# A transformer block of two stages on one core: the rows of x loaded and transposed three weight tiles later, and the modulation chunks weighed on another timetable

## What is computed

```python
c_act = jax.nn.silu(c)
mod = c_act @ w_ada[l] + b_ada[l]                        # (1, 6*2048): shifts, scales, gates
sh1, sc1, gt1, sh2, sc2, gt2 = jnp.split(mod[:, None, :], 6, axis=-1)
h = rmsnorm(x, g_mix[l]) * (1.0 + sc1) + sh1
x = x + gt1 * hybrid_mixer(h, w_in[l], ...)              # pooling, attention, LRU, w_out
h = rmsnorm(x, g_ffn[l]) * (1.0 + sc2) + sh2
x = x + gt2 * conv_glu_ffn(h, ...)
# second block, per layer: memory keys and values
mkv = mem @ w_mem_kv
# keys are normalised per head, transposed, and used by an attention over 256 memory rows
```

## Time and profile before

| | |
|---|---|
| median of 3 runs | 3042.99 us (3042.93 to 3043.94) |
| profiled execution, its own time | 3042.21 us |
| its span in the trace | 3040.4 us |
| TensorE busy | 3020.1 us, 99% |
| VectorE busy | 1970.1 us, 65% |
| ScalarE busy | 1492.6 us, 49% |
| bytes moved | 658.20 MB |

### The profile page before, as it was taken

How to read it: one execution, slowest core, us unless ns; L and a number is a source line. 1 busy time by engine, 2 the same in 40 slices (tenths; PEclk the granted TensorE clock), 3 DMA queues, 4 the chain that set the end, 5 groups by cost and what they waited for, 6 DMA issues and landing times.

```text
span 3040.4 us, 38832 instructions
## 1 busy us (share of the span) xinstructions
PE 3020.1 (99%) x14556; PEld 2533.0 (83%) x14556; DVE 1970.1 (65%) x2078; ACT 1492.6 (49%) x1797; POOL 15.1 (0%) x32
## 2 busy tenths in 40 slices
PE   8999999999999999999999999999999999999999
PEld 6899888888888888888888888888888888888887
DVE  7989987875665568675555656565475555566564
ACT  6555456444444445554444354545454454444543
POOL 0000000000000000000000000000000000000000
PEclk9999999999999999999999999999999999999999
DMA  9998988865555556555555455555455555445454
GB/s 397 416 379 300 365 333 296 311 220 189 190 187 188 189 182 221 175 180 178 190 177 194 161 173 194 174 186 183 163 180 179 193 173 193 166 169 190 170 182 171
DMA packets 167272, 658.20 MB, mean 216 GB/s; under 512 B 18594, under 2 KB 18914, under 8 KB 154722
## 3 DMA queue, kind: packets, MB, share of 16 engines
q1 hardware_dynamic: 163554, 634.85, 59.3%
q0 software_dynamic: 3584, 21.48, 1.9%
HBM read 654.14 MB, written 2.11 MB: 216 GB/s over the span
## 4 chain that ended last, share of the span: by engine, by line
PE 91%; DVE 5%; DMA 3%; ACT 1%; issue 0%; SPq 0%; DVEq 0%; ACTq 0%
PE pg L1194 27%; PE pg L1196 27%; PE pg L1195 27%; DVE R L1765 2%; DMA w_raw<-w 2%; DVE w_lo L1821 2%; PE pm L1229 1%; DMA R<-w_ada 1%; PE pm L1257 1%; PE pm L1652 1%; PE pg L1280 1%; PE pg L1282 1%; PE pg L1281 1%; DVE x_rows L1765 0%; PE pm L1546 0%
## 5 line engine op out<-in xcount | busy, mean ns | idle before, releaser
L1701 DVE TENSOR_TENSOR w_lo<-w_raw,w_hi 128x1024 fp32r<-128x1024 f32 x868 | 1061.3, 1225 | 948.7 <-ACT w_hi L626 944.3
L626 ACT ACTIVATE w_hi<-w_raw 128x1024 fp32r<-128x1024 f32 x868 | 919.7, 1060 | 1294.0 <-PE pg L1196 1287.2
L1194 PE MATMUL pg<-w_hi,hT_hi 128*128 128x512 f32 x2912 | 1146.0, 394 | 4.6 <-DVE w_lo L1821 4.2
L1196 PE MATMUL pg<-w_hi,hT_lo 128*128 128x512 f32 x2912 | 1135.5, 390 | 0.0
L1195 PE MATMUL pg<-w_lo,hT_hi 128*128 128x512 f32 x2912 | 1134.7, 390 | 0.0
L1194 PEld LDWEIGHTS pg<-w_hi,hT_hi 128*128 128x128 f32 x2912 | 547.8, 188 | 120.7 <-issue 5.8
L1196 PEld LDWEIGHTS pg<-w_hi,hT_lo 128*128 128x128 f32 x2912 | 547.3, 188 | 115.1
L1195 PEld LDWEIGHTS pg<-w_lo,hT_hi 128*128 128x128 f32 x2912 | 547.9, 188 | 110.3
L1194 PE MATMUL pg<-w_hi,y_parts 128*128 128x512 f32 x864 | 337.6, 391 | 0.0
L1196 PE MATMUL pg<-w_hi,y_parts 128*128 128x512 f32 x864 | 336.4, 389 | 0.0
L1195 PE MATMUL pg<-w_lo,y_parts 128*128 128x512 f32 x864 | 336.1, 389 | 0.0
(11 more groups left out here) (313 smaller groups left out, 1940.0 us busy)
## 6 DMA issues: line engine op xcount, KB each, us to landing
w_raw<-w SPq DMA_DIRECT2D x1008, 512.0 KB, 4.0
R<-w_ada SPq DMA_DIRECT2D x59, 1024.0 KB, 9.0
x_rows<-w_ada SPq DMA_DIRECT2D x18, 1024.0 KB, 9.1
R<-w_ada POOLq DMA_DIRECT2D x11, 1024.0 KB, 7.3
R<-w SPq DMA_DIRECT2D x16, 512.0 KB, 11.0
R<-w_ada SPq DMA_DIRECT2D x10, 512.0 KB, 7.4
R<-mem_T SPq DMA_DIRECT2D x8, 512.0 KB, 9.2
x_rows<-x SPq DMA_DIRECT2D x4, 1024.0 KB, 13.0
```

The costliest lines, as they stand in the source:

```text
L626: act.activation(w_hi[:, g % RING, :, :].rearrange("p c n -> p (c n)"), raw[:, g % RING, :], ACT.Copy).then_inc(hi_done, 1)
L1194: pe.matmul(out, hi, w_hi[:, slot, c, :], start=start, stop=False)
L1196: return pe.matmul(out, lo, w_hi[:, slot, c, :], start=False, stop=stop)
L1701: tt(flat(w_lo[:, g % RING, :, :]), raw[:, g % RING, :], flat(w_hi[:, g % RING, :, :]).bitcast(F32), ALU.subtract).then_inc(lo_done, 1)
```

## The change

It does six things. (1) X_FROM goes from 14 to 16, and the six places that serve from there on come in the order x, x, 14, 16, 4, 6. (2) WEIGH_FEEDS: sixteen chunks are fed behind tiles 4 to 23 (thirteen behind 5 to 21 before), the other sixteen behind tiles 24 to 43 (nineteen behind 24 to 45 before), and six chunks of a later group go one tile later, behind 114 to 124 instead of 113 to 123. (3) SP loads the two halves of x behind tiles 11 and 13 instead of 7 and 8; ScalarE's squares, VectorE's row_norm and TensorE's transposes of x follow three tiles later. (4) The sums of squares of mk0 are turned into roots before row_norm instead of after it, mem_normed(0) goes from 15 to 17, and the transposes of mk0 from behind tile 16 to behind tile 19; ScalarE's copy of them stays at `upto(21)`. (5) The first two chunks in the buffer of x, now 16 and 17, are loaded at turns 23 and 24 (before: 14 and 15, at turns 22 and 23). (6) TensorE transposes the probabilities of head h one tile later.

```diff
--- before.py
+++ after.py
@@ -29,7 +29,7 @@
 ADA = 6 * D
 AH = D // 2
 X_HOME = 19
-X_FROM, X_TO, X_LEFT = 14, 32, 56
+X_FROM, X_TO, X_LEFT = 16, 32, 56
 RAW_DEEP, RAW_DEEP_TO = RING + 1, 80
 LAYERS = 2
 LEVELS = 9
@@ -89,7 +89,7 @@
     if n < X_FROM:
         first = (14, 16, 4, 6)[n % 4]
     elif n < X_TO:
-        first = (X_HOME, X_HOME + 2, 4, 6, 14, 16)[(n - X_FROM) % 6]
+        first = (X_HOME, X_HOME + 2, 14, 16, 4, 6)[(n - X_FROM) % 6]
     elif n < X_LEFT:
         first = (X_HOME, X_HOME + 2, 14, 16)[(n - X_TO) % 4]
     else:
@@ -477,10 +477,9 @@
 
         P_MEM0, P_MIX, P_Y, P_MEM1, P_FF = 0, 4, 12, 20, 28
         FRONT_SSQ = TB + TB * NB
-        LATE = ((52, 3, 5), (57, 5, 8), (65, 7, 9), (74, 5, 11), (85, 17, 28), (113, 6, 12), (136, 5, 11))
-        FIRST = 13
-        WEIGH_FEEDS = [5, 6, 8, 9] + [11 + 12 * n // 9 for n in range(FIRST - 4)]
-        WEIGH_FEEDS += [24 + 23 * n // (EARLY - FIRST) for n in range(EARLY - FIRST)]
+        LATE = ((52, 3, 5), (57, 5, 8), (65, 7, 9), (74, 5, 11), (85, 17, 28), (114, 6, 12), (136, 5, 11))
+        WEIGH_FEEDS = [4, 5, 6, 7, 9, 10, 12, 13, 14, 15, 17, 18, 19, 20, 22, 23]
+        WEIGH_FEEDS += [24 + 21 * n // (EARLY - X_FROM) for n in range(EARLY - X_FROM)]
         WEIGH_FEEDS += [at + span * i // count for at, count, span in LATE for i in range(count)]
         assert len(WEIGH_FEEDS) == M_GATE2
         SCALED = 6
@@ -495,7 +494,7 @@
             if _n < 4:
                 _turn = (3, 4, 6, 7)[_n]
             elif X_FROM <= _n < X_FROM + 2:
-                _turn = 22 + _n - X_FROM
+                _turn = 23 + _n - X_FROM
             else:
                 _last = ada_before(_n)
                 _turn = turn_after(WEIGH_FEEDS[_last]) if _last < M_GATE2 else None
@@ -544,8 +543,8 @@
                     for at, first, last in ada_loads(n):
                         sp.dma_start(half_slots(at, (last - first) // AH).rearrange("p a d -> p (a d)"),
                                      t["w_ada"][n][:, first:last]).then_inc(ada_in[at], 16)
-                if g in (7, 8):
-                    rows(g - 7)
+                if g in (11, 13):
+                    rows((g - 11) // 2)
                 if g == X_TURN:
                     sp.wait_ge(ada_used, X_LEFT)
                 if g in (X_TURN, X_TURN + 2):
@@ -812,14 +811,13 @@
                         i = act.activation(flat(c_rows)[:, n * NW:(n + 1) * NW], pm[n][:, :], ACT.Silu)
                     i.then_inc(c_ready, 1)
             for tb in range(TB):
-                upto(11 + tb)
+                upto(13 + 2 * tb)
                 act.wait_ge(x_in[tb], 16)
                 squares(tb, x, sq_1)
             row_std(0)
+            head_std(0, 8)
             for q in range(GT):
-                upto(15 + q // 3)
-                if q == 0:
-                    head_std(0, 8)
+                upto(18 + q // 3)
                 rows_T(0, q, 3, hf_1)
             upto(21)
             heads_T(0, (0, 1), mk_T[:, 0, :, :], scale=V("mk_g")[:, 0:1])
@@ -1324,7 +1322,7 @@
                                       start=False, stop=True)
                     i.then_inc(logit_ps, 1)
                 for h in range(NH):
-                    upto(t + 3 + h)
+                    upto(t + 4 + h)
                     pe.wait_ge(exp_done, occ * NH + h + 1)
                     for sb_ in range(TB):
                         for tb in range(TB):
@@ -1340,15 +1338,15 @@
             for n in range(NB):
                 pe.matmul(pm[n][:, :], ones[0:1, :], flat(c_rows)[0:1, n * NW:(n + 1) * NW], start=True, stop=True
                           ).then_inc(c_ps, 1)
-            upto(12)
+            upto(15)
             pe.wait_ge(rows_ready, 1)
             pe.wait_ge(c_ready, 1)
             for q in range(GT):
-                upto((13, 13, 13, 14, 14, 14, 15, 15)[q])
+                upto((16, 16, 16, 17, 17, 17, 18, 18)[q])
                 if q >= 3:
                     pe.wait_ge(hf_done, q - 2)
                 rows_T_normed(q)
-            upto(17)
+            upto(20)
             pe.wait_ge(hf_done, GT)
             pe.wait_ge(hn_ready, 1)
             transposes(mk_tok[0], (0, 1), T_ps)
@@ -1889,7 +1887,9 @@
                     step.settle()
                     tt(spl[:, 4:8], V("lam"), t8[:, 12:16], ALU.min).then_inc(lam_in, 1)
                     step(ts(t8[:, 12:16], t8[:, 12:16], 0.0, None, ALU.max))
-            upto(12)
+            upto(14)
+            mem_squares(0)
+            upto(15)
             row_norm(0, TB)
             dve.wait_ge(con_in, 16)
             step(dve.memset(F_row, 0.0))
@@ -1901,9 +1901,7 @@
                     step.settle()
                 else:
                     i.then_inc(rows_ready, 1)
-            upto(14)
-            mem_squares(0)
-            upto(15)
+            upto(17)
             mem_normed(0)
             upto(20)
             gain_stage(0)
```

## The result

| | before | after |
|---|---|---|
| median of 21 runs each | 3042.93 us (3040.67 to 3044.46) | 3047.81 us (3046.06 to 3050.86) |
| ratio, with its 95% interval | | 1.0017 [1.0011, 1.0023] |
| span of the profiled execution | 3040.4 us | 3045.3 us |

The change costs 4.9 us, in the times as in the spans. The sum had +1.7.

A forecast was written before the change was run, and what follows sets the result against it. TensorE, busy 99% of the span, was taken as the bound, so only its holes could be won. Front +4.5, attention -0.2 and -1.2, late chunks -1.4 gave +1.7 us, so 3044.7 us, range 3038.5 to 3049.5.

The forecast's parts named there:

- Tile 8 and tile 12: Loading x later wins some 3.7 us at tile 8; TensorE waits 3.5 at tile 12, leaving 0.2 us of gain.
- Tiles 13 to 23: TensorE is 2.8 us late at tile 18, then holds 4.5 before tile 23 for the product of mk1's keys.
- The 9.0: TensorE's lateness in us before tile 23, after waiting for the product of mk1's keys at 99.3 us.
- Tiles 24 to 46: VectorE's 63.7 us of work ends at 163.0; TensorE starts tile 45 5.5 us late; +4.5 us taken.
- Transfers don't hold it: For VectorE's tiles 24 to 44: tile 44 comes after 58.5 units of 1024 KB in both orders, about 154 us.
- The bound for the front: Up to tile 51 transfers end at 179.6 against 181.5 us, so the front can win 1.9 us at most.
- Attention: Transposing probabilities one tile later wins 0.2 us in the first attention, given back at tile 79, and 1.2 in the second.
- Late chunks: At tiles 114 to 124, splits pass the later chunks at tiles 116 and 124: 1.4 us won together.
- the list of signs: What the new trace should show, including no wait at tile 116 and a hole of about 3.5 us at tile 12.
- the likeliest case: The whole forecast: 3044.7 us, chance 0.5, its own range 3042 to 3047 us.
- late parts given back: Rival: the front comes out even and the late parts go back to VectorE and the transfers: 3043.0 us, chance 0.15.
- The rivals of the front: Front, faster: VectorE's idle time takes the chunks, 3038.3 us, chance 0.2; slower: tile 23's loss stays, 3049.2 us, chance 0.15.

The follow-up runs named there:

- the copy's run: The changed kernel with ScalarE's copy of mk0's transposed keys one tile later: 3046.6 us, ratio 1.0012.
- the one with both edits: The changed kernel with the sixteen chunks from tile 24 spread by 23 tiles and the copy of mk0's keys two tiles later: 3045.22 us, 1.0007.
- the last run: Changed kernel, chunks from tile 24 spread by 23 tiles, mk0's copy two tiles later, attention edit undone, loads of chunks 19 to 31 two tiles later: 3041.68 us.
- the run in which VectorE was relieved at tiles 43 and 44: The changed kernel with the sixteen chunks from tile 24 on spread by 23 tiles as before, not by 21: 3046.64 us, 1.0010.
- the front alone: The changed kernel with the attention edit and the six later chunks undone: 3046.92 us, ratio 1.0014.

## Why the prediction was right or wrong

- **Tile 8 and tile 12: right.** Tile 8 landed at 32.2 (put at 32.9), the hole there is 0.4; the one at tile 12 is 3.2 (3.5 put down), and nothing of the gain was left. The clock stayed low for 6.8 us, not 3.4, from 1.2 us before TensorE resumed, and TensorE was late by 0.95 at tile 12's end.
- **Tiles 13 to 23: right.** Late by 2.3 at tile 18 (2.8). The split of tile 21 ended at 88.55 (89.3) behind ScalarE's copy, the product of mk1's keys at 98.3 (99.3), the hole is 4.1 (4.5). The 9.0 is the lateness where TensorE resumes; measured there, 8.2. The clock comes on top: put at 1.7, it took 2.6, so that TensorE was late by 10.8 at the end of tile 23 (10.7 with the prediction's own term). Here too the clock was low for 6.8 us.
- **Tiles 24 to 46: the number right.** 63.7 us of VectorE's work; measured 64.7 from 98.3 to 163.04, of which 0.9 are waits. Its end was put at 163.0. That this fits to the tenth is luck: the product came 1.0 us earlier than put, and the work took 1.0 us longer. Late by 4.73, against 4.6 worked out and 4.5 taken. One sentence that fell is "Transfers don't hold it": it looked at tile 44 alone (153.9 before, 154.3 after), but tile 41 lands 7.9 us later than before, because three more chunk loads are ahead of it. In the change this lay just under VectorE's chain; it showed when that got shorter (the copy's run and the one with both edits), and went when the loads were moved (the last run). Another is that the low clock at tile 23 costs nothing further. It is so while VectorE is behind, but without the last chunks' waits TensorE would still be late by 3.1 by its own hole and clock. Nor did I see that the weighing of the last two chunks ahead of tile 44 is itself a cost: the 163.0 has them in, but I took the three chunks fewer as won. The bound for the front has a slip in its sum: 174.2 + 1.06 + 1.22 + 2.9 is 179.4, so that it could win 2.1 us, not 1.9; nothing hangs on it.
- **Attention: mis-sized.** The 0.2 of the first one was near (0.0 measured), and the reason was right: tile 79 gave it all back. The 1.2 of the second is the term that failed. "No split is that close" was read from that stage alone; the split of tile 114, eighteen tiles on, was close enough. The run with this edit alone ends 0.57 late.
- **Late chunks: mis-sized.** 1.4 put down, 0.45 measured alone, since tiles 117 and 125 now wait for the same chunks. In the change tile 116 still waits 0.63 us, where the list of signs had none.
- **The sum.** +4.5 - 2.8 = +1.7; measured +4.7 + 0.2 = +4.9. The direction held, and the range (3038.5 to 3049.5) with 3047.8 in its upper part. Of the likeliest case the front held, but its own range of 3042 to 3047 did not: the late terms, 2.8 us put down as won, are what carries the time out of it. The rival "late parts given back" was right on its second half. It had been coupled to an even front and so had the wrong time.
- **The rivals of the front** were told apart: VectorE's work behind tile 23 took less than 68 us, and the clock's part did not add to the loss in the change itself, where VectorE was as late; it wasn't hidden in the run in which VectorE was relieved at tiles 43 and 44.

What stays open: what decides whether the one wait of 1.9 to 2.0 us at tile 79 is followed by a low clock. It was in three of the seven traces that have it (last chunks spread, mk1's transposes later, x loaded early) and not in the other four, among them the change and attention alone. And how the front's 4.7 us divide between chunks and x has no single answer: alone they give 5.2 and 1.8. With the chunks alone VectorE waits 7.6 us between 30 and 60 us, as it does with x loaded early (7.9), and 5.9 in the change, so the two parts do not simply add up there.

## What to carry to other kernels

Before you count a hole of one engine as won, follow the engine that ends it to its next tight place, however many tiles on; if that engine has no idle time between, the hole is only moved. Where a helper engine's total work up to a point is fixed, add up its idle time and look at what stands last in its row: those two, not the count of jobs moved forward, say when it arrives. And count transfers ahead of every tile of a stretch, not only of its last one.

## What the runs showed of the hardware

The granted clock fell to the lower of its two levels (1.2 and 2.4 GHz) at holes of TensorE, but not for one length. Before, behind 2.45 us of waiting, for 3.4 us. In the change it fell while TensorE still waited, 1.2 us before the end of the waits of 3.22 and 4.08 us, and stayed low for 6.8 us both times. With mk1's transposes later, at tile 12's wait of 3.20 us, it was 3.4 again. And the same hole doesn't always bring it. In the run with attention alone, whose code up to there is that of the kernel before, tile 8 is waited for as long, and the window of the earlier trace rows reads:

```profile
38.00:41.00 3.00, 2.88 (x12) 2.03 (x12) 2.70 (x3) 1.53 (x2) 0.00 (x0) 1.00 1.03 425
```

The run with the late chunks alone has no low clock there either. TensorE is early by 1.5 at the end of tile 8 there, and by nothing at tile 12, where it waits for the split anyway (late by 0.09). In this row of the run with mk1's transposes later it is low behind the wait of tile 79, with TensorE busy throughout:

```profile
287.00:290.00 3.00, 3.00 (x16) 3.00 (x16) 2.97 (x4) 0.00 (x0) 0.00 (x0) 0.51 0.03 11
```

The two holes of attention, 0.9 and 0.7 us, 7.6 us apart, are followed by no low clock in any of the seven traces that have them. Gathered into one of 1.9 to 2.0 us by the attention edit they are in three of seven, and TensorE is later by 1.5 us at the end of tile 79 there.

That this changes from run to run, and not only from kernel to kernel, is what the untraced runs suggest. In 13 of the 21 runs of the change the mean granted clock is 0.997, with a median of 3048.4 us; in the other 8, the traced one among them, it is 0.998 or 0.999, with a median of 3046.9. In the 11 runs of the front alone, which lacks the attention edit, it is never 0.997, and their median is 3046.9 too. A third low stretch in most of the change's runs, at tile 79, would give this; no trace of such a run of the change was kept, so it isn't shown. If it is so, the attention edit did not leave nothing, but cost some of the 4.9 us.
